# A hybrid layer's middle stage: gates in one group, mLSTM in chunks of 128 tokens, all 16 tiles written out

## The reference

```
b = cumsum(log_f);  dmat[t, s] = b[t] - b[s] + log_i[s]   for s <= t
m_t = max(b + m, max_s dmat);  w_inter = exp(b + m - m_t)
s   = (q k^T) * exp(dmat - m_t)
num = w_inter * (C q) + s v;   den = w_inter * (n q) + sum(s)
h   = num / max(|den|, exp(-m_t))
m', C', n' = the state carried to the next chunk: C' = exp(g + m - m') C + sum_s ws[s] v k^T
```

## Time and profile before

| | |
|---|---|
| median of 3 runs | 2543.21 us (2543.1 to 2544.49) |
| profiled execution | 2537.89 us, span 2536.1 us, granted clock 0.956 |
| busy over the span | PE 2265.1 us (89%), DVE 1548.6 (61%), ACT 1051.0 (41%), POOL 566.2 (22%) |

### The profile page before, as it was taken

How to read it: one execution, slowest core, us unless ns; L and a number is a source line. 1 busy time by engine, 2 the same in 40 slices (tenths; PEclk the granted TensorE clock), 3 DMA queues, 4 the chain that set the end, 5 groups by cost and what they waited for, 6 DMA issues and landing times. The chain is left out here.

```text
span 2536.1 us, 51678 instructions
## 1 busy us (share of the span) xinstructions
PE 2265.1 (89%) x21042; PEld 1624.9 (64%) x21042; DVE 1548.6 (61%) x2486; ACT 1051.0 (41%) x2294; POOL 566.2 (22%) x540
## 2 busy tenths in 40 slices
PE   1799999999999981699999999999998399898988
PEld 1576666666666741699898889898997144343333
DVE  6644444443334435567666666666676698888885
ACT  2333333333334322323232222232233388787875
POOL 0600000100000003132333323232323232332331
PEclk9999999999999995899999999999999599999999
DMA  9300000000000007100000000000000802111111
GB/s 397 104 18 18 18 26 18 26 18 18 26 18 18 26 9 296 75 30 25 27 29 29 27 25 26 26 25 25 28 27 16 275 24 67 50 59 59 59 51 50
DMA packets 82220, 138.71 MB, mean 55 GB/s; under 512 B 42433, under 2 KB 63041, under 8 KB 77905
## 3 DMA queue, kind: packets, MB, share of 16 engines
q1 hardware_dynamic: 82000, 135.38, 15.2%
HBM read 103.89 MB, written 31.46 MB: 53 GB/s over the span
## 5 line engine op out<-in xcount | busy, mean ns | idle before, releaser
L1315 PE MATMUL m_bank<-m_arena,m_w_hi 128*128 128x128 bf16 (+1 forms) x2688 | 476.3, 224 | 35.0 <-DVE m_w_lo L1287 20.5
L1316 PE MATMUL m_bank<-m_arena,m_w_hi 128*128 128x128 bf16 (+1 forms) x2688 | 475.9, 221 | 0.0
L1317 PE MATMUL m_bank<-m_arena,m_w_lo 128*128 128x128 bf16 (+1 forms) x2688 | 475.7, 222 | 0.0
L1315 PEld LDWEIGHTS m_bank<-m_arena,m_w_hi 128*128 128x128 bf16 (+1 forms) x2688 | 261.4, 97 | 43.2 <-DVE m_w_lo L1287 20.9
L1316 PEld LDWEIGHTS m_bank<-m_arena,m_w_hi 128*128 128x128 bf16 (+1 forms) x2688 | 266.6, 99 | 0.2
L1317 PEld LDWEIGHTS m_bank<-m_arena,m_w_lo 128*128 128x128 bf16 (+1 forms) x2688 | 260.1, 97 | 0.0
L1705 POOL TENSOR_TENSOR s_hi<-s_sp,s_cols 128x512 bf16<-128x512 f32 x144 | 152.3, 1057 | 364.8 <-DVE s_sp L1836 155.3
L217 POOL TENSOR_TENSOR g_stage<-g_stage,g_nh_row 128x1024 f32<-128x1024 f32 x16 | 52.3, 3269 | 751.0 <-DVE g_stage L486 751.0
L552 PE MATMUL g_bank<-g_h_hi,g_wi_hi 128*128 128x128 bf16 (+1 forms) x1152 | 197.2, 220 | 18.9 <-DVE g_wi_lo L504 18.7
L553 PE MATMUL g_bank<-g_h_lo,g_wi_hi 128*128 128x128 bf16 (+1 forms) x1152 | 196.8, 220 | 0.0
L554 PE MATMUL g_bank<-g_h_hi,g_wi_lo 128*128 128x128 bf16 (+1 forms) x1152 | 196.8, 220 | 0.0
(11 more groups left out here) (357 smaller groups left out, 5663.5 us busy)
## 6 DMA issues: line engine op xcount, KB each, us to landing
m_arena<-in_w_in_dram SPq DMA_DIRECT2D x8, 1604.0 KB, 7.9
g_stage<-in_gla_w_in_dram SPq DMA_DIRECT2D x8, 1544.0 KB, 12.6
g_stage<-in_ada_w_dram SPq DMA_DIRECT2D x8, 1536.0 KB, 11.2
g_xs<-in_x_dram SPq DMA_DIRECT2D x16, 512.0 KB, 3.2
x<-g_stage SPq DMA_DIRECT2D x16, 512.0 KB, 2.7
m_arena<-in_w_mod_dram SPq DMA_DIRECT2D x8, 1024.0 KB, 7.0
m_arena<-x SPq DMA_DIRECT2D x16, 512.0 KB, 3.7
s_xr<-x SPq DMA_DIRECT2D x16, 512.0 KB, 4.1
```

Source lines behind the costliest of these rows:

```text
L1315: pe.matmul(out, l_hi, r_hi, start=(k == 0), stop=False)
L1316: pe.matmul(out, l_hi, r_lo, start=False, stop=False)
L1317: ins = pe.matmul(out, l_lo, r_hi, start=False, stop=(k == n - 1))
```

## The change

- The column order of `w_in` gets 28 zero columns between i and f, so that f begins at row 32 of a result; both gates are one group of 24 matmuls with 36 weight columns.
- The mLSTM runs in chunks of 128 tokens: one `kv`, one `inter`, one state update, one set of gate-row operations per tile. The reset of the cumulative sum and the mask between the halves go.
- Every engine's 16 tiles are written out (`all_tiles(tile)`), no loop is left in the stage.
- `turn_x` of the next tile comes right behind `kv`, ahead of sz, and uses bank B5 in place of G0. `inter` stands between sz and sv. TensorE waits for `hf_done` of the next tile ahead of the window scores, which write B5.
- ACT makes the next x's statistics behind the v copies in place of behind the sq and sk copies; DVE normalises the next x behind `vw`, and makes h ahead of the state update.

```diff
-PARTS = [("i", MH), ("f", MH), ("u", MW), ...
+FROW = 32
+PARTS = [("i", MH), ("pad", FROW - MH), ("f", MH), ("u", MW), ...
-        def all_tiles(eng, tile):
-            tile(0, 0, 0, True, False)
-            with eng.Fori(0, (NT - 2) // 2) as j:
-                tile(2 * j + 1, 1, j, False, False)
-                tile(2 * j + 2, 0, j + 1, False, False)
-            tile(NT - 1, 1, NT // 2 - 1, False, True)
+        def all_tiles(tile):
+            for i in range(NT):
+                tile(i, i % 2, i // 2, i == 0, i == NT - 1)
...
-            pre(pool.memset(keep[:].rearrange("p (c t) -> p c t", t=CH)[:, :, 0:1], 0.0))
-            pre(pool.memset(maskneg[0:CH, CH:T], MASKED))
@@ ACT, tile @@
                 act.activation(av[:, par, :], G1[:, MW:MW + AKV * AD], ACT.Copy).then_inc(s["tv_copied"], 1)
+                if not last:
+                    x_stats(i + 1, 1 - par, half + par, link)
...
-                act.activation(carry[0:MD], TR[0:MD, 4 * MH:6 * MH], ACT.Exp).then_inc(s["cols_exp"], 1)
+                act.activation(carry[0:MD], TR[0:MD, 4 * MH:5 * MH], ACT.Exp).then_inc(s["cols_exp"], 1)
...
-                if not last:
-                    x_stats(i + 1, 1 - par, half + par, link)
                 gate_out("sz", G0, P, (768, 1024), i, par)
@@ DVE, tile @@
-                dve.tensor_scalar(fr, TR[0:MH, T:2 * T], bf_col[0:MH], None, ALU.add).then_inc(s["gates_read"], 1)
+                dve.tensor_scalar(fr, TR[FROW:FROW + MH, 0:T], bf_col[0:MH], None, ALU.add).then_inc(s["gates_read"], 1)
...
-                for ch in range(NC):
-                    ts = slice(ch * CH, (ch + 1) * CH)
-                    link.done(dve.tensor_tensor_scan(m_r[:, ts], g_r[:, ts], g_r[:, ts], m_old[0:MH], ALU.max, ALU.max))
...
+                m_old, m_new = (m_0, m_1) if par == 0 else (m_1, m_0)
+                link.done(dve.tensor_tensor_scan(m_r, g_r, g_r, m_old[0:MH], ALU.max, ALU.max))
+                link.done(dve.tensor_scalar(wi_r, m_r, -1.0, m_old[0:MH], ALU.mult, ALU.add))
+                link.done(dve.tensor_scalar(ws_r, g_r, m_r[:, T - 1:T], None, ALU.subtract))
+                link.done(dve.tensor_tensor(m_new[0:MH], b_r[:, T - 1:T], m_r[:, T - 1:T], ALU.add))
...
                 dve.tensor_tensor(vw, va, s_col.unsqueeze(2).broadcast_to([P, MH, MD + 1]), ALU.mult)\
                    .then_inc(s["vw_done"], 1)
+                if not last:
+                    x_norm(i + 1, 1 - par)
...
-                for ch, bank in enumerate((B3, B5)):
-                    dve.wait_ge(s["kv_done"], NC * i + ch + 1)
...
-                    if ch == 0 and not last:
-                        x_norm(i + 1, 1 - par)
                 if not last:
                     h_make(i + 1)
+                dve.wait_ge(s["kv_done"], i + 1)
+                old, new = C_st[par], C_st[1 - par]
+                for h in range(MH):
+                    ins = dve.scalar_tensor_tensor(new[0:MD, h, :], old[0:MD, h, :], carry[0:MD, h:h + 1],
+                                                   B3[0:MD, h * (MD + 1):(h + 1) * (MD + 1)], ALU.mult, ALU.add)
+                ins.then_inc(s["state_done"], 1)
+                if not last:
                     h_low(i + 1)
@@ TensorE, turn_x @@
-                for n, bank in enumerate((TR, G0)):
+                for n, bank in enumerate((TR, B5)):
...
-                        wait("sz_read", i)
+                        wait("ktok_copied", i)
@@ TensorE, tile @@
-                for n, name in enumerate(("i", "f")):
-                    cs = slice(C0[name], C0[name] + MH)
-                    mm3(TR[0:MH, n * T:(n + 1) * T], [...], "gates_done" if n else None)
+                cs = slice(C0["i"], C0["i"] + FROW + MH)
+                mm3(TR[0:FROW + MH, 0:T], [(w_hi[:, kb, cs], w_lo[:, kb, cs], h_hi[:, kb, :], h_lo[:, kb, :])
+                                           for kb in range(KB)], "gates_done")
...
-                kv(0, B3)
+                pe.wait_ge(s["ktok_copied"], i + 1)
+                pe.wait_ge(s["vw_done"], i + 1)
+                for h in range(MH):
+                    ins = pe.matmul(B3[0:MD, h * (MD + 1):(h + 1) * (MD + 1)], k_tok[:, h, :], vw[:, h, :],
+                                    start=True, stop=True)
+                ins.then_inc(s["kv_done"], 1)
+                if not last:
+                    turn_x(i + 1)
                 pe.wait_ge(s["az_read"], i + 1)
                 by_feature(G0, [(C0["sz"] + n * P, P) for n in range(2)], "sz_done")
-                inter(0)
-                kv(1, B5)
-                if not last:
-                    turn_x(i + 1)
+                wait("state_done", i)
+                for h in range(MH):
+                    ins = pe.matmul(B4[:, h * (MD + 1):(h + 1) * (MD + 1)], qT[0:MD, h, :], C_st[par][0:MD, h, :],
+                                    start=True, stop=True)
+                ins.then_inc(s["inter_done"], 1)
                 pe.wait_ge(s["sqk_copied"], 2 * (i + 1))
                 by_token(G1, C0["sv"], SW, "sv_done")
-                pe.wait_ge(s["state_done"], NC * i + 1)
-                inter(1).then_inc(s["inter_done"], 1)
...
+                pe.wait_ge(s["state_done"], i + 1)
+                if not last:
+                    pe.wait_ge(s["hf_done"], 2 * (i + 2))
                 for head in (0, 1, 2, 4, 5, 3):
```

More of the change, by code:

```diff
@@ L768, in mix_phase @@
         bi_col, bf_col, m_0, m_1 = col(1), col(1), col(1), col(1)
-        g_col, x_col, carry = col(MH), col(3 * MH), col(2 * MH)
+        g_col, x_col, carry = col(MH), col(3 * MH), col(MH)
         w_col, s_col, n_col = x_col[:, 0:MH], x_col[:, MH:2 * MH], x_col[:, 2 * MH:3 * MH]
@@ L867, in tile @@
                 sp.dma_start(sz_d[bass.ds(i * P, P), :], z_sb[par][:, 768:1024]).then_inc(s["sz_out"], 16)
-            all_tiles(sp, tile)
+            all_tiles(tile)
             store_y(NT - 1)
@@ L978, in tile @@
                 pool.tensor_tensor(z_sb[par], z_sb[par], e_sb, ALU.mult).then_inc(s["silu_done"], 1)
-            all_tiles(pool, tile)
+            all_tiles(tile)
             split_y(NT - 1)
@@ L1219, in tile @@
                 dve.wait_ge(s["tv_copied"], i + 1)
-                wait("kv_done", NC * i)
+                wait("kv_done", i)
                 dve.tensor_tensor(vw, va, s_col.unsqueeze(2).broadcast_to([P, MH, MD + 1]), ALU.mult)\
                    .then_inc(s["vw_done"], 1)
+                if not last:
+                    x_norm(i + 1, 1 - par)
                 dve.wait_ge(s["qk_done"], i + 1)
@@ L1302, in _ @@
             dve.wait_ge(s["tiles_free"], 1)
-            all_tiles(dve, tile)
+            all_tiles(tile)
             heads_out(NT - 1, 1)
@@ L1387, in turn_o, with tile @@
                 ins.then_inc(s["oT_done"], 1)
-            def tile(i, par, half, first, last, second=False):
+            def tile(i, par, half, first, last):
+                second = i == 1
                 pe.wait_ge(s["h_lo_done"], i + 1)
-                for n, name in enumerate(("i", "f")):
-                    cs = slice(C0[name], C0[name] + MH)
-                    mm3(TR[0:MH, n * T:(n + 1) * T], [(w_hi[:, kb, cs], w_lo[:, kb, cs], h_hi[:, kb, :], h_lo[:, kb, :])
-                                                      for kb in range(KB)], "gates_done" if n else None)
+                cs = slice(C0["i"], C0["i"] + FROW + MH)
+                mm3(TR[0:FROW + MH, 0:T], [(w_hi[:, kb, cs], w_lo[:, kb, cs], h_hi[:, kb, :], h_lo[:, kb, :])
+                                           for kb in range(KB)], "gates_done")
                 pe.wait_ge(s["hf_done"], 2 * (i + 1))
@@ L1411, in tile @@
                 for h in range(MH):
-                    pe.matmul(TR[0:MD, 4 * MH + NC * h:4 * MH + NC * (h + 1)], sel[:, h, 0:MD],
-                              wi_r[:, CH - 1:T:CH], start=True, stop=True)
+                    pe.matmul(TR[0:MD, 4 * MH + h:4 * MH + h + 1], sel[:, h, 0:MD], wi_r[:, T - 1:T],
+                              start=True, stop=True)
                 for n, row in enumerate((g_r, wi_r, ws_r, nm_r)):
@@ L1493, in _ @@
             pe.wait_ge(s["w_lo"], KB)
-            tile(0, 0, 0, True, False)
-            tile(1, 1, 0, False, False, True)
-            with pe.Fori(1, (NT - 2) // 2) as j:
-                tile(2 * j, 0, j, False, False)
-                tile(2 * j + 1, 1, j, False, False)
-            tile(NT - 2, 0, NT // 2 - 1, False, False)
-            tile(NT - 1, 1, NT // 2 - 1, False, True)
+            all_tiles(tile)
             turn_p(NT - 1, False)
@@ L2031, in _w_in_2_columns @@
     lies["aq"] = lies["aq"].reshape(AKV, AG, AD).transpose(1, 0, 2).reshape(-1)
+    lies["pad"] = _np.full(FROW - MH, at)
     return _np.concatenate([lies[n] for n, _ in PARTS])
```

32 lines of the change are left out of this document (3 added, 29 removed).

## The result

The changed kernel takes 2486.88 us (median of 4 runs, 2483.18 to 2490.13) against 2543.43 (4 runs, 2543.1 to 2544.49): ratio 0.9777, 95% interval 0.9759 to 0.9794, faster. Forecast were 2493.7 us and, for the profiled execution, 2488.4; the profiled one took 2490.13 (span 2488.3 us, granted clock 0.95).

A forecast was written before the change was run, and what follows sets the result against it. TensorE's own instructions were taken to bound stage 2. Products and gates -44.3 us, loop wraps -23.3, new wait +17.6, padded w_in +0.5 gave -49.5: 2493.7 us, range 2474 to 2513.

The forecast's parts named there:

- The bound: Stage 2: a tile costs what its TensorE instructions cost, 56.0 us undisturbed in the kernel before.
- Gates: TensorE's gate matmuls, one group of 24 in place of two: 1.37 us saved a tile.
- State and carried-state products: One 128-token set each in place of two 64-token sets: 0.84 and 0.56 us saved a tile.
- Width decides: New state set priced by its 96 weight columns, not its doubled rows: 0.84 us, as one old set.
- The loop: Stage 2's tiles written out have no loop wraps, so their gaps and clock falls go: 23.3 us saved.
- The wait at P times V: TensorE waits there for ACT's copies of P: 1.17 us a tile, +17.6 us over tiles 1 to 15.
- Clock falls: Stage 2's four falls without a gap, 1.6 us each, stay as they were; no change booked.
- Rival B: The new stall in every tile draws TensorE's clock down to 1.2 GHz: +24 us, 2518 us; chance 0.17.
- A: TensorE stays full in stage 2, no stall at P times V: -67.1 us, 2476 us; chance 0.15.
- C: Straight-line code isn't supplied, an issue gap in every written-out tile: +74 us, 2568 us; chance 0.03.
- D: Weight loads stand out, from the 36-column gates and longer w_hi rows: at most 4 us, 2498 us; chance 0.10.
- From profile to median: The median of runs taken as 5.3 us above the profiled execution: 2488.4 profiled, 2493.7 median.

The follow-up runs named there:

- e2: The changed kernel with the i and f gates again as two groups of 24 matmuls: 2487.91 us, ratio 0.9764.
- e5: The changed kernel with state products using only the first 64 tokens of each tile, same count of products: 2491.18 us (one run).
- e1: The kernel before with stage 2's sixteen tiles written out and nothing else: 2522.41 us, ratio 0.9902.
- e3: The changed kernel with ACT's three copies of P's transposes ahead of the log-sigmoid steps and the mz gate copy: 2462.36 us, ratio 0.9672.
- e10: The changed kernel run again unaltered, in a later session: 2484.43 us, ratio 0.9750.
- e4: The changed kernel with TensorE's spread of the row of maxima moved behind the first az group: 2499.93 us, ratio 0.9798.
- e6: The changed kernel with the carried-state products in two sets of 64 tokens, both from the same state: 2490.86 us (one run).
- e7: The changed kernel with P's copies earlier on ACT and the spread of the row of maxima behind the first az group: 2460.94 us, ratio 0.9653.

## Why the prediction was right, point by point

The mechanism was right, and the sum came close partly by luck: wrong sizes of opposite sign met. In the stretch that the profile shows, from 2536.1 to 2488.3 us, 47.8 us went where 49.5 were forecast. The products of the 128-token chunk gave 12 us more than booked; the clock falls took back 6.4 of it, and the stretches ahead of the first and behind the last set of gate rows, where two profiles of the changed kernel itself differ by 2 to 3 us, came out about 5 us worse than booked.

- **The bound** (TensorE's own instructions, tile by tile): right. All of the gain lies in the distance from 1059.1 to 1874.8.
- **Gates**, 1.37 us a tile: 1.34 of work went. But the prediction booked it as gain, 21.9 us, and the wait as a cost of its own; `e2` shows that in this kernel the two are one: without the merge the time is the same.
- **State and carried-state products**, 1.40 us a tile: mis-sized, 2.17. The tile went from 56.0 to 53.77; with the gates' 1.34 and the wait's 1.27 that leaves 2.17 us for them, 12 us more than booked in sixteen tiles. The step that failed was to price the new sets from rows of sets that stand beside products of another size, and to put the neighbours at nothing. Read from start to start, in the kernel before (the earlier trace rows has the rest):

```profile
1299.50 1.11 PE L1441 MATMUL m_bank<-m_arena 96*128 96x128 f32 x8
1300.54 0.92 PE L1449 MATMUL m_bank<-m_arena 64*96 64x97 f32 x8
1301.39 0.23 PE L1315 MATMUL m_bank<-m_arena,m_w_hi 128*128 128x128 bf16 x1
...
1304.20 0.30 PE L1455 MATMUL m_bank<-m_arena 96*64 96x97 f32 x1
...
1306.79 0.27 PE L1315 MATMUL m_bank<-m_w_hi,m_arena 128*128 128x256 bf16 x1
```

  and in the changed kernel, behind the lines shown with `e5`:

```profile
1458.23 1.08 PE L1439 MATMUL m_bank<-m_arena 96*128 96x97 f32 x8
1459.15 0.28 PE L1298 MATMUL m_bank<-m_w_hi,m_arena 128*128 128x256 bf16 x1
...
1461.78 1.03 PE L1446 MATMUL m_bank<-m_arena 128*128 128x97 f32 x8
1462.74 0.37 PE L1462 MATMUL m_bank<-m_arena 64*128 64x128 f32 x1
```

  The new state set takes 0.68 us (booked 0.84; I chose between ends of 0.84 and 1.06, and it lay under both), the new carried-state set 0.92 (booked 1.06). Five neighbours that were booked at nothing got shorter: the q k^T set 1.04 to 0.94, the transposes of x 0.93 to 0.88, the sz group 2.81 to 2.70, the sv group 2.72 to 2.63, the masked scores times v 1.06 to 0.96, together 0.45 us. With 1.01 and 0.71 for the sets themselves that is the 2.17. "Width decides" held for the spacing inside a set, which `e5` shows to be the same at 64 and 128 rows; what it left out is the change of size at a set's edges, 0.31 us for one set of 64 rows (`e5`).
- **The loop**, 23.3 us: right; `e1` alone gives 25.6.
- **The wait at P times V**, 1.17 us a tile: right in place, cause and size (1.27). `e3` removes exactly its cause.
- **Clock falls**, four kept: the places were right, the number wrong. Eight (seven at the gate rows, one behind the first full wait): 6.4 us more than booked. That TensorE's work and order at the gate rows were unchanged was no reason for the same count; with tiles of 56.0 us the fall came in four of fifteen, with 53.8 in every second one. Why the count follows the tile's length is not shown.
- **Rival B** (the wait draws the clock down): I gave it 0.17 and it did not come in the changed kernel, but for one tile (two in `e10`). `e4` shows that it is real: the same wait of 1.1 us, and nine tiles with a fall behind it. The argument against it, that only gaps of 3 us did this, was wrong.
- **Rivals A, C, D**: A's time, 2476, needs the wait gone; `e3` goes under it. C: the most "issue" in stage 2 of any written-out version is 1.8 us in all, eight times 0.2, in `e4`. D: the gate group starts at 1465.27 and the u group at 1466.73, 1.46 us where the two groups took 2.80, so the 24 matmuls that went were worth 56 ns each; nothing of D is seen.
- **From profile to median**: the profiled execution was 5.3 us under the median before and 3.3 above it after. Taking the offset of one kernel over to the other made 8.6 us of error, more than the sum had.

## What to carry to other kernels

Where an engine is full, follow each chain that leaves it and comes back, and compare its length with the engine's work in between: that slack, here 1.0 us, is all that fewer instructions in between can bring; what is cut beyond it comes back as a wait, and an order on another engine's queue that shortens the chain (here three copies moved ahead of one that waits for a reciprocal, 24.5 us less in `e3` than in the changed kernel) can then be worth more than the cut.
Price a set of small products together with its neighbours: here a full-size set among full-size ones cost less (0.68 us) than any row of a set that stood beside another size (0.84 and more), and its neighbours got shorter too.
Don't carry a count of clock falls over to a kernel whose period has changed; take away the wait and the thin stretch together, or count on the falls to move.

## What the runs showed of the hardware

- Eight products of 64 rows amid 128-row ones cost TensorE 0.31 us more than the same eight with 128 rows: 0.10 at the set ahead, 0.16 at the set's own edges, 0.05 behind (`e5`). For 64 weight columns beside 128 the group ahead took 0.1 us more (`e6`). The Trainium skill (TensorEngine Tiling (Array Packing), section Key Properties) says that changing the tiling mode drains TensorE, and that different tiles can run in parallel. The traces here agree with both, the first by the 0.31 us of `e5`, the second by the two sets of `e6`, whose products start in turns and take 1.21 us together where one by itself took 0.81; that these products are run as tiles is not shown by a run.
- The granted clock fell to its lower level, 1.2 GHz, with TensorE busy throughout, at the narrow products of the gate rows, and behind waits of 1.1 us (`e4`); with neither it stayed at 2.4 GHz for 769 us (`e7`). Each fall cost 1.6 to 1.7 us or twice that.
- A wrap of the two-tile loop left TensorE without instructions for 2.7 to 3.1 us, five times of five; written out (`e1`), the same tiles have no wait from 1080 to 1850 us.
